# The even layer's attention in a two-block model: one block of projections or of the pools' output in each step, single buffers, small products between

## The reference

```python
n = rms_norm(h, g);  q, k, v, f, u = split(n @ w_in)          # 3*512 + 8 + 512 columns
q, k = rms_norm(q, q_g), rms_norm(k, k_g)                      # over each head's 64
c = cumsum(log_sigmoid(f + b_f))                               # 8 heads
for each block of 128 queries, each head:                      # causal
    s = q_blk @ k.T / 8 + c_q - c_k;  s = where(mask, s, -inf)
    att = softmax(s) @ v
pool_g = (windowed mean of u_g over 2, 4, 8, 16 tokens - u_g) @ w_pool_g * pool_scale
h = h + concat(att, pool) @ w_out
```

## Time and profile before

| | |
|---|---|
| three runs | 1962.27 to 1963.08 us, median 1962.77 us |
| the profiled execution | 1960.69 us, with a span of 1958.9 us from its first to its last instruction |
| busy, share of the span | PE 97%, DVE 62%, ACT 41% |
| DMA | 160.69 MB in all, mean 82 GB/s |
| TensorE clock granted, mean | 0.984 of full speed |

### The profile page before, as it was taken

The page is one execution under the profiler, slowest core; times in us unless marked ns, Lnnn a source line. Parts: engine busy times, 40 slices in busy tenths (PEclk is TensorE's granted clock), DMA queues, the critical chain, the costliest instruction groups (busy, mean ns, idle before and its releaser), DMA issues.

```text
span 1958.9 us, 21827 instructions
## 1 busy us (share of the span) xinstructions
PE 1891.2 (97%) x8620; PEld 1532.1 (78%) x8620; DVE 1220.4 (62%) x1750; ACT 797.5 (41%) x1286; POOL 0.2 (0%) x4
## 2 busy tenths in 40 slices
PE   8999899999999999988799999999999899999999
PEld 6766789788888888755588888888788688888887
DVE  5566666577777444635477777533988667777521
ACT  4137410454444333234454444323755554444311
POOL 0000000000000000000000000000000000000000
PEclk9999999999999999997899999999999999999999
DMA  6211110232222233210032232223111032222222
GB/s 225 86 54 65 49 28 1 64 120 97 97 97 95 90 96 117 92 32 17 28 124 97 97 98 94 100 93 101 54 44 54 11 108 97 97 97 97 94 95 80
DMA packets 48918, 160.69 MB, mean 82 GB/s; under 512 B 5552, under 2 KB 6192, under 8 KB 48688
## 3 DMA queue, kind: packets, MB, share of 16 engines
q1 hardware_dynamic: 48816, 159.29, 24.6%
HBM read 157.17 MB, written 2.10 MB: 81 GB/s over the span
## 4 chain that ended last, share of the span: by engine, by line
PE 90%; ACT 5%; DVE 4%; issue 1%; DMA 0%; DVEq 0%; SPq 0%; ACTq 0%
PE bank L156 89%; ACT mixer_arena L625 2%; ACT wh L625 1%; DVE mixer_arena L1040 1%; DVE mixer_arena L1048 1%; DVE even_arena L1534 1%; DVE wl L1040 1%; ACT even_arena L625 0%; PE bank L516 0%; DVE even_arena L1044 0%; ACT L625 0%; DVE even_arena L1048 0%; ACT conf_diag_l L625 0%; ACT conf_diag_h L625 0%; ACT sq L625 0%
## 5 line engine op out<-in xcount | busy, mean ns | idle before, releaser
L625 ACT ACTIVATE wh<-raw 128x1024 fp32r<-128x1024 f32 (+2 forms) x310 | 308.9, 999 | 790.0 <-PE bank L156 777.1
L156 PE MATMUL bank<-nh,wh 128*128 128x512 f32 x1520 | 602.4, 396 | 11.4 <-DVE nl L1048 8.2
L156 PE MATMUL bank<-nh,wl 128*128 128x512 f32 x1520 | 593.2, 390 | 0.0
L156 PE MATMUL bank<-nl,wh 128*128 128x512 f32 x1520 | 592.9, 390 | 0.0
L1040 DVE TENSOR_TENSOR wl<-raw,wh 128x1024 fp32r<-128x1024 f32 (+2 forms) x310 | 355.7, 1148 | 287.3 <-ACT wh L625 286.5
L156 PEld LDWEIGHTS bank<-nh,wh 128*128 128x128 f32 x1520 | 286.2, 188 | 76.6 <-DVE wl L1040 8.5
L156 PEld LDWEIGHTS bank<-nl,wh 128*128 128x128 f32 x1520 | 286.2, 188 | 63.3 <-issue 4.3
L156 PEld LDWEIGHTS bank<-nh,wl 128*128 128x128 f32 x1520 | 286.0, 188 | 60.3
L156 PE MATMUL bank<-ff_yh,wh 128*128 128x512 f32 x528 | 205.4, 389 | 0.0
L156 PE MATMUL bank<-ff_yl,wh 128*128 128x512 f32 x528 | 205.4, 389 | 0.0
L156 PE MATMUL bank<-ff_yh,wl 128*128 128x512 f32 x528 | 205.4, 389 | 0.0
(11 more groups left out here) (191 smaller groups left out, 1802.5 us busy)
## 6 DMA issues: line engine op xcount, KB each, us to landing
raw<-in_ff_a_up SPq DMA_DIRECT2D x44, 512.0 KB, 3.3
raw<-in_ff_b_up SPq DMA_DIRECT2D x44, 512.0 KB, 3.2
raw<-in_ff_c_up SPq DMA_DIRECT2D x44, 512.0 KB, 3.2
raw<-in_w_in SPq DMA_DIRECT2D x32, 512.0 KB, 3.3
raw<-in_pw SPq DMA_DIRECT2D x24, 512.0 KB, 3.3
raw<-in_even_in SPq DMA_DIRECT2D x16, 512.0 KB, 3.3
raw<-in_ff_a_down_a SPq DMA_DIRECT2D x8, 512.0 KB, 3.2
raw<-in_ff_a_down_b SPq DMA_DIRECT2D x8, 512.0 KB, 3.2
```

The costliest lines, as they stand in the source:

```text
L156: return e.matmul(out, lhsT, rhs, start=start, stop=stop, skip_group_check=True)
L625: return e.activation(out, in_, func, **kw).then_inc(n.give(sem), 1)
```

## The change

v's token pieces come first, then f, k0, q0, u0; the nine other projections and the eight blocks of out_pool become the covers of the attention's steps, one block in each of eighteen slots, with none in slot 12. Small products (`forget`, `att_sum`, `pooled`) go one at a time to bank 7 between them, from the lists EARLY and LATE. Scores run no step ahead; s, nmax, sum and rsum are single, p is double; flip runs one slot behind and output two. The blocks of the slots alternate between banks 0 and 1, and 2 and 3 hold the scores, 4 and 5 the transposes, 6 the output. The sums of k and q take two buffers instead of eight, `mixed` one instead of four, `pool` two instead of four. The layer's four constant loads move on SP's queue from the place of piece 4 to that of piece 9 of the layer, and `even_select` has 8 partitions instead of 128.

```diff
+EVEN_BLOCKS = (("k", 0), ("q", 0), ("u", 0), ("k", 1), ("q", 1), ("u", 1), ("u", 2), ("k", 2), ("q", 2), ("u", 3), ("k", 3), ("q", 3))
+FILL = EVEN_BLOCKS[3:] + (("out", 0), ("out", 1), ("out", 2), None, ("out", 3), ("out", 4), ("out", 5), ("out", 6), ("out", 7))
+SLOTTED = len(FILL)
+STEPS = HEADS * TB
+EARLY = {0: ("forget", 2), 1: ("norm", 2), 2: ("norm", 3), 3: ("forget", 3), 4: ("forget", 4), 5: ("norm", 4), 6: ("norm", 5),
+         7: ("forget", 5), 8: ("norm", 6), 9: ("norm", 7), 10: ("forget", 6), 11: ("forget", 7)}
+LATE = {2: 0, 4: 1, 6: 2, 8: 3}
+POOLS = {0: 0, 3: 1, 5: 2, 7: 3}
...
+    def small_product(lhsT, rhs, done, read, j=7):
+
+        if j == 7:
+            e.wait_ge(*small["read"])
+            small["read"] = read
+        else:
+            vacate(j)
+        mm(bank[j][:, :], lhsT, rhs, True, True).then_inc(n.give(done), 1)
...
     def scores(s):
         p, t = att[s]
-        if s >= 2:
-            e.wait_ge(c.scored, 2 * (s - 1))
+        if t == 0:
+            e.wait_ge(c.att_scaled, 2 * p + 2)
+        if s == 0:
+            e.wait_ge(c.forget_read, 2)
+        else:
+            e.wait_ge(c.scored, 2 * s)
...
+    def fill(i, j):
+        take(j)
+        if FILL[i][0] == "out":
+            piece(j, m2.yph, m2.ypl, range(HEADS), ready=c.pool_low if FILL[i][1] == 0 else None)
+        else:
+            piece(j, c.nh, c.nl, range(DK))
+
+    j = 0
+    for i in range(SLOTTED):
+        if FILL[i] and i < SLOTTED - 1:
+            j = 1 - j
+            fill(i, j)
+        if i in EARLY:
+            (forget if EARLY[i][0] == "forget" else att_sum)(EARLY[i][1])
+        if i < STEPS:
+            scores(i)
+        if 1 <= i <= STEPS:
+            flip(i - 1)
+        if i >= 2:
+            output(i - 2)
+        if i in LATE:
+            pooled(LATE[i])
+    fill(SLOTTED - 1, 1 - j)
```

ACT's and DVE's loops over the slots:

```diff
+    for i in range(SLOTTED):
+        if i in EARLY:
+            (forget if EARLY[i][0] == "forget" else att_root)(EARLY[i][1])
+        if 1 <= i <= STEPS:
+            turn(i - 1)
+        if i < STEPS:
+            softmax(i)
+        if FILL[i]:
+            if i < SLOTTED - 1:
+                feed()
+                group()
+            if FILL[i][0] in "kq":
+                att_square(2 * FILL[i][1] + (FILL[i][0] == "q"))
+        if i - 2 >= 0 and (i - 2) % TB == TB - 1:
+            pair_high((i - 2) // TB)
+        if i in LATE:
+            pool_high(LATE[i])
...
+    for i in range(SLOTTED):
+        if FILL[i] and i < SLOTTED - 1:
+            j = 1 - j
+            even_block(*FILL[i], j)
+        if i in EARLY and EARLY[i][0] == "forget":
+            forget(EARLY[i][1])
+        if i < STEPS:
+            softmax(i)
+        if i in EARLY and EARLY[i][0] == "norm":
+            att_scale(EARLY[i][1])
+        if i < STEPS:
+            normed(i)
+        if FILL[i] and i < SLOTTED - 1:
+            feed()
+        if i in POOLS:
+            pool(POOLS[i])
+        if i - 2 >= 0 and (i - 2) % TB == TB - 1:
+            pair_low((i - 2) // TB)
+        if i in LATE:
+            pool_low(LATE[i])
...
-        if s == even + 4:
-            e.wait_ge(c.block_done, even)
+        if s == even + 9:
+            e.wait_ge(c.block_done, even + 3)
```

More of the change, by code:

```diff
@@ L453, in tensor_program @@
     feed_forward(1)
-    def att_sum(i):
-        e.wait_ge(c.att_squared, i + 1)
[L458 to L464, removed]
+    small = dict(read=None)
+    def small_product(lhsT, rhs, done, read, j=7):
[5 more added lines that the diff above has]
+        mm(bank[j][:, :], lhsT, rhs, True, True).then_inc(n.give(done), 1)
@@ L466, in pooled, with att_sum, forget @@
+    def att_sum(i, j=7):
+        e.wait_ge(c.att_squared, i + 1)
+        small_product(m2.half_ones, m2.hsq[i % 2], c.att_summed, (c.att_logged, i + 1), j)
+    def forget(h, j=7):
+        e.wait_ge(c.f_rows, 1)
+        small_product(m2.select[:, h * P:(h + 1) * P], m2.rows[0:AH, :], c.forget_done, (c.forget_read, h + 1), j)
     def pooled(g):
         e.wait_ge(c.mixed_ready, g + 1)
-        if g >= 2:
-            e.wait_ge(c.pool_low, g - 1)
-        mm(bank[4 + g % 2][:, :], m2.wpool[:, g, :], m2.mixed[:, g, :], True, True).then_inc(n.give(c.pooled), 1)
@@ L472, in tensor_program, with second_sum @@
[L472 to L477, removed]
+        small_product(m2.wpool[:, g, :], m2.mixed, c.pooled, (c.pool_low, g + 1))
+    def second_sum(w):
+        if w == 1:
             token_sums(2)
+            vacate(6)
             e.wait_ge(c.accb_done, DK - 1)
             mm(bank[6][:, :], c.ones[:, :], m2.accb, True, True).then_inc(n.give(c.stat_done), 1)
-        if b == 4:
+        else:
@@ L482, in tensor_program @@
             e.wait_ge(c.both_roots, 1)
             root_columns(7)
[L484 to L487, removed]
-    att = [(p, t) for p in range(HEADS) for t in range(TB)]
[L492 to L498, removed]
+    token_pieces(c.nl_ready, 2 * DK, {1: (1,), 3: (3,)}, second_sum)
@@ L500, in scores @@
+    take(4)
+    piece(4, c.nh, c.nl, range(DK))
+    take(5)
+    piece(5, c.nh, c.nl, range(DK))
+    take(6)
+    piece(6, c.nh, c.nl, range(DK))
+    e.wait_ge(c.even_ready, 16 * 4)
+    small["read"] = (c.rcol_ready, 2)
+    att_sum(0)
+    forget(0, 2)
+    take(0)
+    piece(0, c.nh, c.nl, range(DK))
+    att_sum(1, 4)
+    forget(1, 3)
+    att = [(p, t) for p in range(HEADS) for t in range(TB)]
     def scores(s):
         p, t = att[s]
-        if s >= 2:
-            e.wait_ge(c.scored, 2 * (s - 1))
+        if t == 0:
[4 more added lines that the diff above has]
+            e.wait_ge(c.scored, 2 * s)
@@ L526, in output @@
                 lo = q * AD
-                done = mm(bank[1][lo:lo + AD, t * P:(t + 1) * P], m2.v[:, j, p * P + lo:p * P + lo + AD],
+                done = mm(bank[6][lo:lo + AD, t * P:(t + 1) * P], m2.v[:, j, p * P + lo:p * P + lo + AD],
                           m2.pt[s % 2][q][:, j * P:(j + 1) * P], j == 0, j == t)
         done.then_inc(n.give(c.att_done), 1)
[L531 to L552, removed]
+    def fill(i, j):
+        take(j)
+        if FILL[i][0] == "out":
+            piece(j, m2.yph, m2.ypl, range(HEADS), ready=c.pool_low if FILL[i][1] == 0 else None)
+        else:
+            piece(j, c.nh, c.nl, range(DK))
[15 more added lines that the diff above has]
+    fill(SLOTTED - 1, 1 - j)
     for m in range(DK):
@@ L891, in scalar_program @@
             act(m2.q1, m2.q1, ACT.Exp, c.root_done, scale=-0.5)
[L892 to L904, removed]
@@ L905, in scalar_program @@
-    for w in range(RING):
-        feed()
[L907 to L925, removed]
+    e.wait_ge(c.rcol_done, 2)
@@ L927, in softmax @@
+    act(c.rcol[:, :], bank[7][:, 0:TB], ACT.Copy, c.rcol_ready)
+    feed()
+    e.wait_ge(c.f_for_act, 1)
+    act(m2.ln[0:AH, :], m2.az[0:AH, :], ACT.Exp, c.act_step, scale=-1.0)
+    settle()
+    act(m2.ln[0:AH, :], m2.ln[0:AH, :], ACT.Ln, c.f_logged, bias=1.0)
+    at["group"] += TB + 1
+    for i in range(2):
+        feed()
+        group()
+        att_square(i)
+    att_root(0)
+    forget(0, 2)
+    feed()
+    group()
+    att_root(1, 4)
+    forget(1, 3)
     def softmax(s):
-        p, t = att[s]
@@ L950, in scalar_program @@
[L950 to L963, removed]
+        act(m2.yah[:, p, :], bank[6][:, :], ACT.Copy, c.att_hi)
+    for i in range(SLOTTED):
[7 more added lines that the diff above has]
+            if i < SLOTTED - 1:
+                feed()
+                group()
+            if FILL[i][0] in "kq":
[4 more added lines that the diff above has]
+            pool_high(LATE[i])
@@ L1475, in vector_program @@
         arrive()
[L1476 to L1484, removed]
-            tt(z, bank[0][0:AH, :], c.r[0:AH, :], ALU.mult, c.evac)
-        else:
-            scaled((m2.k if b < 9 else m2.q)[:, (b - 5) % HEADS, :], b % 4)
@@ L1510, in vector_program @@
-        if b in (6, 8, 10, 12):
-            pool_low((b - 6) // 2)
+        if name == "out":
+            add_block(j, k)
+        else:
+            scaled(dict(k=m2.k, q=m2.q)[name][:, k, :] if name != "u" else m2.pool[:, k % 2, 16:], j)
     for w in range(RING):
@@ L1801, in build @@
         B = arena(ctx, "even", 0, arena=([P, ARENA], F32))["arena"]
-        behind = 44 * S + 4 * (16 + S)
-        small, at = {}, behind + 2 * (16 + S)
-        for name, w in dict(causal=P, sums=P + len(WINDOWS) * 16, qs=1, nmax=4, sum=6, rsum=4, part=2).items():
+        small, at = {}, 49 * S
+        for name, w in dict(causal=P, sums=P + len(WINDOWS) * 16, qs=1, nmax=2, sum=2, rsum=2, part=2).items():
             small[name] = B[:, at:at + w]
             at += w
-        for name in ("nmax", "sum", "rsum"):
-            small[name] = small[name].rearrange("p (r q) -> p r q", q=2)
@@ L1825, in build @@
+            wpool=B[:, 50 * S:51 * S].rearrange("p (k s) -> p k s", s=P), accb=ff.accb,
+            half_ones=small["sums"][:, 0:P], count=small["sums"][:, P:], **small,
```

(2 more changed lines are left out.)

238 lines of the change are left out of this document (118 added, 120 removed).

## The result

The changed kernel takes 1928.52 us (median of four runs, 1927.23 to 1929.06) against 1962.52 before: a ratio of 0.9827, 95% interval [0.9811, 0.9842]. The forecast was 1929. The profiled execution took 1928.18 with a span of 1926.4, 32.5 less than before.

The account below looks back on a forecast made before the run. PE bounds the kernel, but the 214.5 us stage loses 48.9 to idle time and half clock. Floor 165.6, waits 7.9, clock 4 and slips 3 put out_att at 941, 34 earlier: 1926.7, forecast 1929 by the median; range 1920 to 1946.

Parts of the forecast that it names:

- The floor: PE's own work at full clock from the first projection to out_att, the same before and after: 165.6 us.
- Waits: PE's waits over the attention's steps in the new order: five waits, 7.9 us in sum.
- The 1.8 for pool_low: At the turn from projections to out_pool, PE waits 1.8 us for pool_low before out_pool 0's last quarter.
- the 0.4 for bank 7: In step 4 PE waits 0.4 us because bank 7 is still read by forget(4).
- the 1.5 for flip(15): In step 16 flip(15) waits 1.5 us for the weights of t = 3.
- step 12: The step without a cover block: its scores and flip(11) wait, 3.6 us together.
- Clock: One fall of PE's clock over a starved stretch around steps 11 to 12: 0 to 8 us, taken as 4.
- Slips: Changes between fp32r blocks and small products, and semaphore delays the hand schedule rounds off: 0 to 6 us, taken as 3.
- Case D: Cover fails: single buffers put the whole round trip behind the block, 4.5 us in each of 16 steps: 1986; chance 0.05.
- Rival A: PE's clock swings all through from step 0 on, staying at 0.80 despite little idle time: 1949; chance 0.08.
- Rival B: The last nine steps are bound by the round trip, 12 us more plus a clock fall: 1941 to 1945; chance 0.13.
- case C: No stall: arrival at the floor 1914, or 1921 with half the slips and no clock fall; chance 0.09.

Follow-up runs that it names:

- hole9: The changed kernel with the empty slot moved from 12 to 9 and the last three small products one slot later: 1922.36 us, 0.9795 of the kernel before.
- nolag: hole9 with each flip in its own step's slot, right behind the scores, and outputs one slot behind: 2003.91 us, 1.0207 of the kernel before.
- run 124: Not a follow-up run: words of "let PE run 124 us without a pause", a length of time in hole9, whose measured time is 1922.36 us.
- old_late: The kernel before with the forget row taken one step later on DVE, behind the next step's weight scaling: 1962.05 us, 0.9994 of the kernel before.
- dve_more: hole9 with three more DVE products of 320 columns in each step, between reciprocals and scaling: 1936.32 us.
- Body: The changed kernel with nine projections before the steps, which keep only out_pool blocks, placed as in the kernel before: 1942.23 us, 0.9902 of the kernel before.

## Why the prediction was right, step by step

**The floor and the stage.** Predicted: 165.6 us of PE's work, out_att at 941, 180 us after the stage's start. Measured: 941.16 and 178.5. PE is unbroken to step 8, waits stand only at steps 9 and 12, and the clock is over 0.95: all as forecast. That out_att starts at 941 to the tenth is luck: the stage is 2 us shorter than the sum and began 1.6 later in this execution. (The stage before began at 761.13, the first row, and not at 760.9; the product of 760.90 belongs to the feed-forward.)

**Three terms of the sum were off, and cancelled.** *Waits:* 7.9 forecast, 2.6 measured. The 1.8 for pool_low was 0.2 in the record, the 0.4 for bank 7, the 0.6 for pooled(3) and the 1.5 for flip(15) weren't there, and step 12 cost 2.4 and not 3.6. *Clock:* 4 forecast for one fall, 1.7 measured (0.65 over 914 to 918, 0.92 over the next four). *Slips:* 3 forecast; 178.5 - 165.6 - 2.6 - 1.7 leaves 8.6. This term is the one that was mis-sized, nearly threefold.

hole9 says where these 8.6 us are. It has no wait and no fall, and its stage takes 174.1 us, 8.5 above the floor, so the surplus is in PE's own stream. Taken from the start of each kind of product to the start of the next, the 25 blocks take 119.1 us instead of 115.1, the outputs 11.2 instead of 8.8, the flips 10.9 instead of 9.6, and all else 32.9 instead of 32.1. The floor's rates for outputs and flips were read from steps of four key blocks, where the change is spread over many products. From its first slot (812.1) to out_att hole9 makes about eighty changes; at 0.12 each they are 10 us, an upper estimate, since some of the floor's terms already hold one.

This surplus may also explain why the waits were fewer: the block of step 7 ended at 879.4 instead of 874, about 4 us of it from the slower stream, and a PE that is slower than planned waits less for DVE and ACT. That is argued and was not tried. It would mean that such errors in a hand schedule lean against each other.

**Single buffers cost nothing.** This was right where measured (hole9 has no wait for scored or for bank 7's reader), and nolag shows the condition: the chain must be split over two blocks. Case D's price was 4.5 us a step, all of it waiting and with the turning in it; nolag cost 5.1 a step, of which 3.4 are waits, so the two numbers are close only because the clock made up the difference.

**The rule on rotating banks** (the Trainium skill, "Perfetto Trace Analysis", Optimizing Tensor Performance, Matmuls) didn't decide here: two banks in turn for the blocks and one for all small products let PE run 124 us without a pause. The trace of old_late agrees with the rule: a block waits 2.14 us for the reader of a small product in its own bank.

**Rival A** (the Trainium skill, "TensorE: Matmul & The Clock Gate", A second HAM failure mode: psum-queue depth-cycling) didn't come in the changed kernel, since small products without idle time between didn't lower the clock at all: 1.00 over hole9's 124 us. **Rival B** didn't come either: steps 9 to 16 show waits at step 12 alone, but for the 0.20 at pool_low. But dve_more shows that the last steps are close to bound by the chain. By its own figures B was priced too low as well: 5.2 and a block of 2.8 against 4.9 is 3.1 more a step, 25 us in eight and not 12, which would lie beyond the range. The 1921 of case C doesn't follow from its sum either; 1929 less 4 and 1.5 is 1923.5.

**What I had wrong without paying for it:** I read the stage as lacking covers alone. Body shows that the order itself (v first, a lag of one slot, small products in a bank of their own, all together) is worth 20 us. The prediction doesn't mention the longest wait of the stage before, 3.98 us at the start of the attention with a clock of 0.58 over 28 us. How the 20 divide between the start and the steps stays open. The move of the four loads and the smaller select were not tried alone; PE doesn't wait in the projections after the change (51.00 of 51 us busy), so they cost nothing there.

## What to carry to other kernels

When PE alternates long blocks with a chain through other engines, put the block between the chain's start and the product that needs its end; depth of buffers comes after that, and here one set for the scores and sums was enough. Leave an empty slot behind the shortest step, not the longest. Before a wait is worth removing, look at whether the stage then really idles less at the same clock: a partial repair can be taken back whole.

## What the runs showed of the hardware that I had not expected

Idle time of PE cost more than its length. Held against hole9's stage, the kernel before lost 40.2 us with 24.1 idle, nolag 82.8 with 53.8, the changed kernel 4.4 with 2.6, between 1.5 and 1.7 times the idle time; hole9 has no idle time and a clock of 1.00. And a change between kinds of product (blocks in fp32r, small fp32 products, transposes, outputs) costs about 0.12 to 0.15 us even when nobody waits, so that how finely PE's work is interleaved has a price of its own, most of 8.5 us here.
